# Two RWKV-7 buffers of a hybrid decoder kernel, run half a round apart

## The chip, the cores and the metric

One NeuronCore of a Trainium2 chip runs the whole program. The metric is device time in microseconds, the median of three runs. TensorE multiplies matrices, VectorE, ScalarE and GpSimd (POOL) work element by element, and each of them executes its own queue strictly in the order of the program. SyncE issues the weight transfers. The engines meet only through semaphores: an instruction that waits holds up everything behind it on its engine.

## What is computed

A decoder trunk of two layers on 256 prompt tokens and 8 sequences of 8 new tokens (T = 320 columns). The even layer has HGRN2 heads and RWKV-7 heads side by side; the change concerns the RWKV-7 heads alone. Per token:

```python
def rwkv7_scan(r, w, k, v, kk, a, s0):
    def step(s, inp):
        r_t, w_t, k_t, v_t, kk_t, a_t = inp
        sa = jnp.einsum('bhij,bhj->bhi', s, -kk_t)
        s = (s * w_t[:, :, None, :] + sa[..., None] * (kk_t * a_t)[:, :, None, :]
             + v_t[..., None] * k_t[:, :, None, :])
        return s, jnp.einsum('bhij,bhj->bhi', s, r_t)
```

Ahead of it stand the low-rank products for the decay, `a` and the gate (sigmoids), a normalised `kk` (square root and reciprocal) and exponentials; behind it a group norm (square root and reciprocal), a bonus term and the gate. There are 16 heads of 64; the last state of each head is written back for the prompt and for each of the 8 sequences.

## The kernel before

The program is written engine by engine. Weight products fill most of the time: every weight tile is split in a high and a low part (`split_hi`, `split_lo`, L280 and L291) and multiplied in three passes (L316, L320). Between the input projection of the even layer with its HGRN2 heads and the output projection `out_even` lies a stretch in which only the RWKV-7 heads run. This stretch is what the change touches.

The 16 heads are 8 tiles of two heads (128 partitions). Two tiles make a group (RJ = 2), there are four groups, and two sets of buffers, `rbuf[0]` and `rbuf[1]`, each with its own tiles, its own semaphores and four PSUM banks. A buffer does one group in one round, and two rounds in all. The 320 columns are five chunks of 64: four of the prompt, one that holds the eight sequences. One round of one buffer has 74 stages (RSTAGES):

- The front, stages 0 to 8. TensorE: low-rank products `lora` (L1237, L1238), sums of squares (L1244), bonus (L1249). ScalarE: sigmoids (L1005, L1006), square root (L1013), exponentials (L1017 to L1019). VectorE: a first block (L1093 to L1102), a block with a reciprocal (L1105 to L1107), four products that end in `tB` (L1111 to L1120). POOL: one product (L1222).
- Transposes and Gram products, stages 8 to 16. TensorE: 30 transposes (L1265), evacuated by ScalarE and VectorE in turns (L1074), then L1280 and L1277, masked by VectorE (L1129), and five operations that set up the inverse (L1138 to L1143).
- Five rungs of a triangular inverse, stages 16 to 36. A rung is a product (L1308), its copy to T1 by ScalarE (L1035), the next mask by VectorE (L1152), two more products (L1316, L1318; the fifth has L1316 alone) and additions by VectorE (L1158, L1161).
- Five chunks in sequence, stages 36 to 62. Each has three products on TensorE (`rhs` L1346, `sa` L1356, `ys` from L1365) with copies by ScalarE between them (L1046, L1049, L1053), and a state update by VectorE (L1172 to L1175). Ahead of the last one the states of the eight sequences are read (L1336).
- The tail, stages 62 to 74. New states of the sequences (L1378, L1380; VectorE L1183 to L1196), the group norm (L1387, L1393, square root L1065 on ScalarE, reciprocal L1206 on VectorE and what follows it up to L1214) and the gate (L1397).

Each engine's part is a generator (`rwkv_pe`, `rwkv_act`, `rwkv_dve`, `rwkv_pool`) that yields the stage of what it issues next. `by_stage` merges the generators of both buffers: it always takes the one with the lowest stage, and buffer 0 at a tie. As the stages of both buffers are equal, every step of buffer 0 is followed on its engine by the same step of buffer 1. The second round begins at stage 74 with a wait for the buffer's own `end` and, on ScalarE, for its stores (`rwkv_act`). After the stretch ScalarE and TensorE wait for the end of both buffers before `out_even` begins.

Of the kernel before, what the change touches and what calls it, by code (L numbers as in the profile page):

```python
# [109 lines left out]
def build(nc, d):  # L110
# [5 lines left out]
    with ctx:  # L116
# [282 lines left out]
        def part(ap, c):  # L399
            return ap[:, 2 * c:2 * c + 2, :]  # L400
# [140 lines left out]
        def by_stage(*programs):  # L541


            ahead = [[next(p, None), p] for p in programs]
            while any(a[0] is not None for a in ahead):
                a = min((a for a in ahead if a[0] is not None), key=lambda a: a[0])
                a[0] = next(a[1], None)


        HG, HGROUPS, HSTAGES = 2, 4, 21  # L550
        hK = at("hK", HT0, [P, HG, T])
# [665 lines left out]
        def rwkv_pool(pool, x):  # L1217
            r = rbuf[x]
            for G in range(RGROUPS // 2):
                yield G * RSTAGES + 6  # L1220
                r.wait(pool, "b", G + 1)
                pool.tensor_tensor(r.tB[:, :, :], r.KK[:, :, :], r.A[:, :, :], mult).then_inc(r.sem("kka"), 1)  # L1222
# [553 lines left out]
        @block.sync  # L1776
        def _(sp):
            for name in ORDER:
                ring_load(sp, plan[name])

        @block.gpsimd
        def _(pool):
            split_head(pool, "pool", plan["in_a"])
            pre_norm_pool(pool, FILL[0])
            pool_split(pool, plan["in_a"], skip=HEAD)
            in_b_pool(pool)
            by_stage(rwkv_pool(pool, 0), rwkv_pool(pool, 1))
            split_head(pool, "pool", plan["out_even"])
            mixer_x_pool(pool, FILL["mix0"])
            pool_split(pool, plan["out_even"], skip=HEAD)  # L1790
            split_head(pool, "pool", plan["up00"])
            post_norm_pool(pool, 1)
            channel_pool(pool, 0, plan["in_c"])
            pre_norm_pool(pool, FILL[4])
            pool_split(pool, plan["in_c"], skip=HEAD)
            pool_split(pool, plan["in_d"])
            split_head(pool, "pool", plan["out_odd"])
            mixer_x_pool(pool, FILL["mix1"])
            pool_split(pool, plan["out_odd"], skip=HEAD)
            split_head(pool, "pool", plan["up10"])  # L1800
            post_norm_pool(pool, 5)
            channel_pool(pool, 1, None)

        @block.scalar
        def _(act):
            act.dma_start(com[:, :], d["common"]).then_inc(sem("com_in"), 16)
            for c in range(8):
                act.dma_start(part(X, c), d["x"][:, 2 * c:2 * c + 2]).then_inc(sem(f"x_in{c}"), 16)
            act.dma_start(vecs[:, :], d["vecs"]).then_inc(sem("vecs_in"), 16)
            act_head(act, plan["in_a"])  # L1810
            act.wait_ge(sem("com_in"), 16)
            pre_norm_act(act, 0)

            for dst, src in ((hgm_in[:, :, :], "hgm"), (evc[:, :], "evc"), (sh_in[:, :, :], "shift_in")):
                act.dma_start(dst, d[src]).then_inc(sem("even_consts"), 16)
            act_split(act, plan["in_a"], skip=HEAD)
            by_stage(fill_act(act), hgrn_act(act))
            shift_act(act)
            by_stage(rwkv_act(act, 0), rwkv_act(act, 1))
            for r in rbuf:  # L1820
                act.wait_ge(r.sem("end"), 2)
                act.wait_ge(r.sem("store"), 64)
            act_head(act, plan["out_even"])
            mixer_x_act(act)
            act.wait_ge(sem("stored"), 16)
            act.dma_start(X[:, :, :], d["x"]).then_inc(sem("x_reload"), 16)
            act_split(act, plan["out_even"], skip=HEAD)
            act_head(act, plan["up00"])
            root_act(act, 1)
            channel_act(act, 0)  # L1830
            act_head(act, plan["in_c"])
            root_act(act, 3)
            pre_norm_act(act, 4)

            act.dma_start(x_spill, X[:, :, :]).then_inc(sem("spilled"), 16)
            act.wait_ge(sem("spilled"), 16)
            for dst, src in ((odc[:, :], "odc"), (cv_in[:, :, :, :], "conv_in"), (h_in[:, :, :], "h_in"),
                             (w_a[:, :, :, :], "w_a"), (w_x[:, :, :, :], "w_x")):
                act.dma_start(dst, d[src]).then_inc(sem("odd_consts"), 16)
            act_split(act, plan["in_c"], skip=HEAD)  # L1840
            by_stage(odd_fill_act(act), rglru_act(act))
            ret_act(act)
            act.wait_ge(sem("mix1_end"), 1)
            act_head(act, plan["out_odd"])
            mixer_x_act(act)
            act.wait_ge(sem("stored"), 16 * 3)
            act.dma_start(X[:, :, :], x_spill).then_inc(sem("x_reload"), 16)
            act_split(act, plan["out_odd"], skip=HEAD)
            act_head(act, plan["up10"])
            root_act(act, 5)  # L1850
            act.wait_ge(sem("ret_store3"), 32)
            channel_act(act, 1)
            root_act(act, 7)
            for c in range(8):
                x_new_wait(act, 7, c)
                act.dma_start(d["y"][:, 2 * c:2 * c + 2], part(X, c)).then_inc(sem("stored"), 16)
            act.wait_ge(sem("stored"), 16 * 11)
            act.wait_ge(sem("hgrn_store"), 32 * HGROUPS)

        @block.vector  # L1860
        def _(dve):
            split_head(dve, "dve", plan["in_a"])
            dve.wait_ge(sem("vecs_in"), 16)
            pre_norm_dve(dve, 0, ("mix_pre", 0), FILL[0])
            evacuate(dve, plan["in_a"], Z, skip=HEAD)
            dve.wait_ge(sem("even_consts"), 16 * 3)
            link(dve, "dve", dve.tensor_copy(hgm[:, :, :], hgm_in[:, :, :]))
            for g in range(HGROUPS):
                hgrn_dve(dve, g)
            dve.wait_ge(sem("shifted"), 26)  # L1870
            by_stage(rwkv_dve(dve, 0), rwkv_dve(dve, 1))
            pass_over(dve, plan["in_b"])
            split_head(dve, "dve", plan["out_even"])
            x_lo_dve_half(dve, mixer_part, FILL["mix0"])
            evacuate(dve, plan["out_even"], M, stats=1, skip=HEAD)
            split_head(dve, "dve", plan["up00"])
            post_norm_dve(dve, 1, ("mix_post", 0))
            channel_dve(dve, 0, plan["in_c"])
            pre_norm_dve(dve, 4, ("mix_pre", 1), FILL[4])
            evacuate(dve, plan["in_c"], Z[:, 32:48, :], skip=HEAD)  # L1880
            rglru_dve(dve)
            rotate_dve(dve)
            ret_dve(dve)
            pass_over(dve, plan["in_d"])
            split_head(dve, "dve", plan["out_odd"])
            x_lo_dve_half(dve, mixer_part, FILL["mix1"])
            evacuate(dve, plan["out_odd"], M, stats=33, skip=HEAD)
            split_head(dve, "dve", plan["up10"])
            post_norm_dve(dve, 5, ("mix_post", 1))
            channel_dve(dve, 1, None)  # L1890

        @block.tensor
        def _(pe):
            pe.wait_ge(sem("com_in"), 16)
            pre_norm_pe(pe, 0)
            multiply(pe, plan["in_a"], x_hi, x_lo, FILL[0])
            pe.wait_ge(sem("tile_out"), 32)
            by_stage(fill_pe(pe), hgrn_pe(pe))
            pe.wait_ge(sem("tile_out"), EVEN_TILES)
            pe.wait_ge(sem("hgrn_end"), HGROUPS)  # L1900
            pe.wait_ge(sem("lora_in"), 1)
            pe.wait_ge(sem("lora_w"), 32)
            by_stage(rwkv_pe(pe, 0), rwkv_pe(pe, 1))
            for r in rbuf:
                pe.wait_ge(r.sem("end"), 2)
            multiply(pe, plan["out_even"], x_hi, x_lo, FILL["mix0"])
            post_norm_pe(pe, 1)
            channel_pe(pe, 0)
            pre_norm_pe(pe, 4)
            multiply(pe, plan["in_c"], x_hi, x_lo, FILL[4])  # L1910
            pe.wait_ge(sem("tile_out"), plan["in_d"].tile0)
            by_stage(odd_fill_pe(pe), rglru_pe(pe))
            ret_pe(pe)
            pe.wait_ge(sem("mix1_end"), 1)
            multiply(pe, plan["out_odd"], x_hi, x_lo, FILL["mix1"])
            post_norm_pe(pe, 5)
            channel_pe(pe, 1)
# [93 lines left out]
```

## Time and profile before

| | us |
|---|---|
| median of the runs shown | 3699.97 (3682.28 to 3700.11, n = 3) |
| span of the profiled execution | 3677.0 |
| RWKV-7 stretch in it, first `lora` product to the end | 608.04 to 921.50 |

The span runs from the first to the last instruction; the profile gives no other time of that execution, and the runs are measured outside it. A row of the windows below gives busy time and, in brackets, the instructions of TensorE's products, its weight loads, VectorE, ScalarE and POOL, then the share of full speed that TensorE's clock was granted (1.00 is 2.4 GHz, 0.50 is 1.2 GHz), the DMA share and GB/s. In the timeline an instruction's row is its start, its length, engine, line, operation, what it writes and reads, shape and count, and in brackets the idle time of its engine before it with what ended that.

### The profile page before, as it was taken

What the parts mean: (1) busy time and instruction counts of PE and PEld (TensorE: products, weight loads), DVE (VectorE), ACT (ScalarE), POOL (GpSimd) and SP (SyncE); (2) the same over time, 40 slices, a digit from 0 to 9 for tenths busy, and PEclk for the clock granted to TensorE, in tenths of its full rate; (3) what the DMA queues carried; (4) which work ended last, traced back from release to release, by engine and by line L of the source; (5) the groups of instructions that cost most, each with busy time, mean ns of one, the idle gap of its engine ahead of it and who ended that gap; (6) DMA issues with size and microseconds to landing.
All of it is one profiled execution on the core that took longest, in us unless ns stands there. A gap on an engine that the chain in (4) does not pass through costs nothing.

```text
span 3677.0 us, 63816 instructions
## 1 busy us (share of the span) xinstructions
PE 3407.4 (93%) x24784; PEld 3270.7 (89%) x24784; DVE 1678.0 (46%) x2251; ACT 1169.2 (32%) x1384; POOL 1643.6 (45%) x1038
## 2 busy tenths in 40 slices
PE   7998896857879999999999799998979999999997
PEld 7998885846879999999999699985979999999997
DVE  3236667485563332233334546814563332233345
ACT  3244443231333332233322235421233332233322
POOL 4556773000444444544444455721444445444443
PEclk9999997978889999999999899986989999999999
DMA  5443331000424444444443444542424444444442
GB/s 166 151 150 111 122 105 55 4 24 15 153 88 149 148 150 159 137 149 148 148 159 133 148 145 124 173 144 120 145 91 148 148 155 154 137 149 148 155 150 107
DMA packets 118658, 474.81 MB, mean 129 GB/s; under 512 B 13425, under 2 KB 15089, under 8 KB 115569
## 3 DMA queue, kind: packets, MB, share of 16 engines
q1 hardware_dynamic: 108864, 421.58, 35.8%
q10 hardware_dynamic: 9648, 51.17, 3.6%
q8 instruction: 107, 1.75, 0.2%
q14 instruction: 39, 0.31, 0.0%
HBM read 450.66 MB, written 22.03 MB: 129 GB/s over the span
## 4 chain that ended last, share of the span: by engine, by line
PE 86%; DVE 9%; ACT 2%; issue 1%; POOL 1%; DMA 1%; ACTq 0%; DVEq 0%; POOLq 0%
PE ps L316 50%; PE ps L320 25%; DVE M L462 1%; PE ps L1719 1%; PE ps L1739 1%; DVE xn L425 1%; PE ps L837 1%; PE ps L1316 1%; POOL x_lo L433 1%; PE ps L418 0%; PE ps L1318 0%; PE ps L1280 0%; DVE Z L718 0%; PE ps L1265 0%; PE ps L1482 0%
## 5 line engine op out<-in xcount | busy, mean ns | idle before, releaser
L291 POOL TENSOR_TENSOR w_lo<-raw,w_hi 128x512 fp32r<-128x512 f32 (+2 forms) x756 | 1463.6, 1937 | 1734.7 <-ACT w_hi L280 1733.9
L316 PE MATMUL ps<-x_hi,w_hi 128*128 128x320 f32 x5024 | 1515.7, 315 | 89.8 <-POOL x_lo L433 71.8
L316 PE MATMUL ps<-x_lo,w_hi 128*128 128x320 f32 x5024 | 1504.1, 313 | 0.0
L280 ACT ACTIVATE w_hi<-raw 128x1024 fp32r<-128x1024 f32 (+1 forms) x756 | 840.8, 1113 | 1654.3 <-PE ps L320 1618.2
L316 PEld LDWEIGHTS ps<-x_hi,w_hi 128*128 128x128 f32 x5024 | 959.8, 191 | 107.9 <-issue 73.6
L291 DVE TENSOR_TENSOR w_lo<-raw,w_hi 128x512 fp32r<-128x512 f32 (+1 forms) x640 | 515.8, 807 | 1030.0 <-ACT w_hi L280 1012.1
L316 PEld LDWEIGHTS ps<-x_lo,w_hi 128*128 128x128 f32 x5024 | 961.8, 191 | 0.6
L320 PE MATMUL ps<-x_hi,w_lo 128*128 128x320 f32 x5024 | 846.4, 311 | 1.9 <-POOL w_lo L291 1.9
L320 PEld LDWEIGHTS ps<-x_hi,w_lo 128*128 128x128 f32 x5024 | 769.5, 189 | 2.9 <-POOL w_lo L291 2.9
L316 PE MATMUL ps<-u_hi,w_hi 128*128 128x320 f32 x1408 | 415.5, 310 | 6.3 <-DVE u_lo L530 6.3
L316 PE MATMUL ps<-u_lo,w_hi 128*128 128x320 f32 x1408 | 415.1, 309 | 0.0
L316 PEld LDWEIGHTS ps<-u_hi,w_hi 128*128 128x128 f32 x1408 | 264.4, 188 | 7.3 <-DVE u_lo L530 7.3
L316 PEld LDWEIGHTS ps<-u_lo,w_hi 128*128 128x128 f32 x1408 | 264.4, 188 | 0.0
L320 PE MATMUL ps<-u_hi,w_lo 128*128 128x320 f32 x1408 | 227.4, 309 | 0.0
L320 PEld LDWEIGHTS ps<-u_hi,w_lo 128*128 128x128 f32 x1408 | 211.8, 188 | 0.0
L530 DVE TENSOR_TENSOR u_lo<-stat,u_hi 128x320 f32 (+1 forms) x88 | 131.8, 1498 | 10.1
L523 DVE TENSOR_TENSOR stat<-gate,ps 128x320 f32<-128x320 f32 x88 | 42.9, 488 | 172.2 <-PE ps L320 172.2
L510 ACT ACTIVATE gate<-ps 128x320 f32<-128x320 f32 x88 | 38.5, 437 | 221.1 <-PE ps L320 221.1
L343 DVE COPY M<-ps 128x320 f32 (+1 forms) x64 | 31.5, 492 | 157.4 <-PE ps L320 157.4
L1222 POOL TENSOR_TENSOR tB<-rKK,rA 128x640 f32<-128x640 f32 x4 | 6.5, 1619 | 191.4 <-DVE rKK L1107 191.4
L418 PE MATMUL ps<-sq,com 128*128 128x320 f32 x128 | 46.9, 527 | 38.7 <-ACT sq L408 38.7
L418 PEld LDWEIGHTS ps<-sq,com 128*128 128x128 f32 x128 | 28.1, 231 | 57.0 <-ACT sq L408 36.5
(359 smaller groups left out, 2606.9 us busy)
## 6 DMA issues: line engine op xcount, KB each, us to landing
raw<-in_w_ffn_in SPq DMA_DIRECT2D x352, 512.0 KB, 3.5
raw<-in_w_ffn_out SPq DMA_DIRECT2D x128, 704.0 KB, 4.0
raw<-in_w_in_even SPq DMA_DIRECT2D x116, 512.0 KB, 3.5
raw<-in_w_in_odd SPq DMA_DIRECT2D x96, 512.0 KB, 3.5
raw<-in_w_out_even SPq DMA_DIRECT2D x32, 512.0 KB, 3.5
raw<-in_w_out_odd SPq DMA_DIRECT2D x32, 512.0 KB, 3.5
hS<-in_state_hgrn ACTq DMA_DIRECT2D x4, 1024.0 KB, 5.5
out_hgrn_s<-hS ACTq DMA_DIRECT2D x4, 1024.0 KB, 4.9
```

The costliest lines, as they stand in the source:

```text
L280: nc.scalar.activation(w_hi[s % 2][:, 0:g.kt, :], raw[s % 4][:, 0:g.kt, :], ACT.Copy)\
L291: eng.tensor_tensor(w_lo[s % 2][:, k0:k1, :], raw[s % 4][:, k0:k1, :], w_hi[s % 2][:, k0:k1, :].bitcast(f32), sub).then_inc(sem(f"split_lo ...
L316: nc.tensor.matmul(out, w_hi[s % 2][:, k, :], x[:, kk, :], start=half == 0 and k == 0 and x is xh, stop=False)
L320: mm = nc.tensor.matmul(out, w_lo[s % 2][:, k, :], xh[:, half * g.kt + k, :], start=False, stop=half == 1 and k == g.kt - 1)
L418: ins = nc.tensor.matmul(PS[7][:, 0:T], ones, sq[:, k, :], start=k == 0, stop=k == KT - 1)
L425: ins = dve.scalar_tensor_tensor(xn[:, k, :], X[:, k, :], vec(w[0], KT * w[1] + k), stat[:, 1, :], mult, mult)
L433: eng.tensor_tensor(part(x_lo, c), src, part(x_hi, c).bitcast(f32), sub)\
L462: ins = dve.scalar_tensor_tensor(M[:, k, :], M[:, k, :], vec(w[0], KT * w[1] + k), stat[:, 1, :], mult, mult)
L510: nc.scalar.activation(gate[:, p % 2, :], PS[(g.tile0 + 2 * p) % 4][:, 0:T], ACT.Silu)\
L523: dve.tensor_tensor(uf, gate[:, p % 2, :], PS[(g.tile0 + 2 * p + 1) % 4][:, 0:T], mult)\
L530: dve.tensor_tensor(lo, uf, hi.bitcast(f32), sub).then_inc(sem("u_lo"), 1)
L837: ins = mm(PS[b0][:, o:o + P], x[:, j, cs], x[:, j, cs], start=True, stop=True)
```

## The change

`by_stage` itself stays. The generators of the RWKV-7 stretch are wrapped in `paced`, which turns a stage into a position on a scale of 115 units per round, by straight lines between the points of PACE, and adds half a round (57.5) to all positions of buffer 1. Stage 0 is at 0, stage 8 at 21, 16 at 33, 36 at 63, 62 at 95, 74 at 115. All four engines are merged by these positions. No instruction, tile, wait or semaphore is added or removed.

```diff
+        PACE = ((0, 0), (8, 21), (16, 33), (36, 63), (62, 95), (74, 115))
+
+        def paced(program, late):
+
+            for stage in program:
+                G, n = divmod(stage, PACE[-1][0])
+                k = max(k for k, (first, _) in enumerate(PACE[:-1]) if first <= n)
+                (n0, t0), (n1, t1) = PACE[k], PACE[k + 1]
+                yield late * PACE[-1][1] / 2 + G * PACE[-1][1] + t0 + (n - n0) * (t1 - t0) / (n1 - n0)
...
-            by_stage(rwkv_pool(pool, 0), rwkv_pool(pool, 1))
+            by_stage(*(paced(rwkv_pool(pool, x), x) for x in range(2)))
...
-            by_stage(rwkv_act(act, 0), rwkv_act(act, 1))
+            by_stage(*(paced(rwkv_act(act, x), x) for x in range(2)))
...
-            by_stage(rwkv_dve(dve, 0), rwkv_dve(dve, 1))
+            by_stage(*(paced(rwkv_dve(dve, x), x) for x in range(2)))
...
-            by_stage(rwkv_pe(pe, 0), rwkv_pe(pe, 1))
+            by_stage(*(paced(rwkv_pe(pe, x), x) for x in range(2)))
```

## Rows read from the trace of the kernel before

**Rows 1.** The page: span, and shares of the chain that ended last.

```profile
span 3677.0 us, 63816 instructions
PE 86%; DVE 9%; ACT 2%; issue 1%; POOL 1%; DMA 1%; ACTq 0%; DVEq 0%; POOLq 0%
```

**Rows 2.** Windows: from:to and length, then the columns above; front, Gram, stretch.

```profile
608.04:637.88 29.84, 10.36 (x32) 5.80 (x32) 25.11 (x34) 12.67 (x22) 3.21 (x2) 0.61 0.09 30
637.88:662.22 24.34, 19.60 (x300) 18.66 (x301) 20.16 (x38) 7.77 (x20) 0.00 (x0) 0.92 0.01 1
608.04:921.50 313.46, 222.26 (x4136) 189.60 (x4136) 200.40 (x321) 81.33 (x187) 6.48 (x4) 0.83 0.05 15
```

**Rows 3.** Waits of TensorE in the stretch: who, us in total, times, longest.

```profile
PE ps L1265 <- DVE tB L1120: 33.1, 2, 16.7
```

**Rows 4.** Timeline of VectorE in the front of round 1.

```profile
617.21 0.68 DVE L1093 TENSOR_SCALAR tAR<-rA,vecs 128x320 f32<-128x320 f32 x2
622.02 0.49 DVE L1105 TENSOR_SCALAR rE<-rE 128x640 f32<-128x640 f32 x1
627.48 0.48 DVE L1105 TENSOR_SCALAR rE<-rE 128x640 f32<-128x640 f32 x1
632.93 1.68 DVE L1111 TENSOR_TENSOR BV<-ps,Z 128x320 f32<-128x320 f32 x4
```

**Rows 5.** Chain of waits, round 1 (start, us, what): transposes, Gram products, last rung.

```profile
637.88 8.39 PE ps L1265 x60
...
649.97 2.62 PE ps L1280 x48
652.59 0.93 PE ps L1277 x32
...
655.50 1.77 PE ps L1280 x32
...
698.99 1.88 PE ps L1316 x64
```

**Rows 6.** Timeline of the rungs of round 1.

```profile
666.40 2.40 PE L1308 MATMUL ps<-XI,NTm 64*64 64x64 f32 x40 [1.77 <-DVE XI L1143]
668.84 0.77 ACT L1035 ACTIVATE T<-ps 128x512 f32<-128x512 f32 x2 [3.41 <-PE ps L1308]
...
672.73 0.69 DVE L1158 TENSOR_TENSOR XT<-XT,ps 128x512 f32<-128x512 f32 x1 [3.06 <-PE ps L1318]
...
674.13 0.28 DVE L1161 TENSOR_TENSOR XI<-XI,ps 128x128 f32<-128x128 f32 x1
...
676.96 1.38 PE L1308 MATMUL ps<-XI,NTm 64*64 64x64 f32 x40 [0.77 <-DVE XI L1161]
...
684.97 1.15 PE L1308 MATMUL ps<-XI,NTm 64*64 64x64 f32 x32 [1.00 <-DVE XI L1161]
```

**Rows 7.** Windows, columns as in the second group: rungs before and after the clock rose, tail.

```profile
662.22:672.02 9.80, 8.03 (x145) 7.84 (x147) 5.67 (x7) 1.53 (x4) 0.00 (x0) 0.50 0.01 2
672.02:701.00 28.98, 26.00 (x859) 25.51 (x857) 16.74 (x32) 5.12 (x10) 0.00 (x0) 1.00 0.01 4
731.00:756.87 25.87, 17.08 (x104) 8.92 (x100) 19.87 (x30) 5.37 (x10) 0.00 (x0) 0.90 0.12 47
```

**Rows 8.** Chain of waits, round 1: state products, the last VectorE block of either buffer.

```profile
722.31 6.58 PE ps L1336 x122
...
749.19 4.16 DVE ySQ L1206
...
756.82 4.07 DVE ySQ L1206
```

**Rows 9.** Timeline of ScalarE: first and last of seven table loads, and an activation.

```profile
615.30 1.28 ACT L1013 ACT_TABLE_LOAD   x1
616.59 1.42 ACT L1013 ACTIVATE rE<-ps 128x320 f32<-128x320 f32 x4
...
904.04 1.28 ACT L1065 ACT_TABLE_LOAD   x1
```

## The prediction

> **What bounds the kernel now.** I read the page first: the chain that ended last lies on TensorE for 86% of a span of 3677.0 us [rows 1], so this is a kernel bound by its weight products. The change touches none of them, only the RWKV-7 stretch, so I then read that stretch by windows: it runs from the first lora product at 608.04 to 921.50, 313.5 us, and TensorE is busy for 222 of them, VectorE for 200 [rows 2]. Neither is full: a round of both buffers is some 157 us, with TensorE busy 111 and VectorE 100. The wait view tells where the difference goes: TensorE stands for 33.1 us in two waits for `tB`, the last operation of the front [rows 3], while VectorE does reciprocals; in the rungs it is VectorE's turn to wait. So the stretch alternates between a front of 29.84 us on VectorE (25.11 busy), and rungs on TensorE (26.00 of 28.98 at the full clock) [rows 2, 7]. Running one buffer's front beside the other's rungs is then a fair idea; the question is what a single buffer's chain costs and what the merged queues let it do.
>
> **How I sum.** In the new order the buffers' steps are sorted by PACE positions on every engine. Buffer 1's first product (L1237, stage 1) has position 57.5 + 2.6 = 60.1; buffer 0's fifth rung has 58.5 (L1308, stage 33) and 61.5 (L1316, stage 35). So on TensorE's queue buffer 1 starts right behind L1308 of buffer 0's last rung. Half a round on, the same three positions come with the roles exchanged (116, 117.6, 119), and again at 173.5 and 175.1. TensorE executes in order, therefore each half-round is at least as long as one buffer's path from its lora products to its fifth rung. Call it S, and E what is left behind that, from the fifth rung to the end. The stretch is S alone, three times S with the other buffer's E put between its steps (S + x), and E alone: **4 S + 3 x + E**, against 313.5 us now. The two halves of PACE's round look equal on paper; the sum asks for S, not for their mean.
>
> **S, one buffer alone.** Front: 29.84 us for both [rows 2]. Of buffer 1's VectorE work two blocks lie in it ahead of buffer 0's next step, from 617.21 to 622.02 (4.81) and from 627.48 to 632.93 (5.45) [rows 4]; without them 19.6. Transposes and Gram products: 24.34 us [rows 2], of which half of the 8.39 us of transposes and buffer 1's Gram products, 2.62 + 0.93 + 1.77 = 5.3, are the other buffer's [rows 5]: 14.8. Rungs: one is L1308 (1.38 us), the copy of T1 on ScalarE (0.77), 80 products of L1316 and L1318 at 1.88 / 64 = 0.029 us (2.35) [rows 5], four additions on VectorE from 672.73 to 674.41 (1.7) [rows 6]; with some 0.5 for the hand-overs 6.7 us. The third and fourth have 8 blocks in place of 10 and one bank, 5.4 (an estimate by these rates); with L1308 of the fifth, 2 x 6.7 + 2 x 5.4 + 1.2 = 25.4. **S = 19.6 + 14.8 + 25.4 = 60** at the full clock. The telling comparison is here: a rung of both buffers takes 8.0 us (676.96 to 684.97 for buffer 1's second) [rows 6], hardly more than one of a single buffer. Lockstep already hides the hand-overs of one buffer under the products of the other.
>
> **The clock.** After the idle time ahead of the first rung the rows show a granted clock of 0.50 (1.2 GHz) for 9.8 us, in which TensorE was busy for 8.03; then 1.00 (2.4 GHz) while it was busy nine tenths of the time [rows 7]. L1308 takes 2.40 us at the lower level, 1.38 at the higher [rows 6], a factor of 1.74. Alone, a rung has TensorE busy for 3.7 of its 6.7 us, a smaller share than in either of these rows, so I expect the first S to run at the lower level in part. Its 15 us of rung products would grow by 11, the transposes and Gram products by up to 8: S lies between 60 and 79, and I take 70 for the first. In the shared halves TensorE has more to do, and I keep 60.
>
> **x, what the other buffer adds.** Its E lies between the steps of S, in order on every queue. Nothing (0) if all of it falls into idle time, all of E (47) if nothing does. By place: (1) its last VectorE block, from 749.19 to 756.82, 7.6 us [rows 8], has position 111.7, ahead of the fourth rung's additions (114.5); those are ready some 3 us into it, so 4.5. (2) Its tail has 17.08 / 2 = 8.5 us of products [rows 7] spread over rungs 1 to 3, which leave TensorE idle for 3 us each; but each step waits in order for its own additions or copies: 4. (3) Chunks 3 and 4 and the state products (6.58 / 2 = 3.3 us for L1336 [rows 8]) stand among transposes, Gram products and the first rung, where TensorE is itself on the chain: 7.5 us of products, of which 6.5 count. (4) Chunks 0 to 2 beside the front: VectorE's state updates and the first waits, 3. **x = 18**, between 12 and 24.
>
> **E alone.** The rest of the fifth rung 2.5; four chunks at 4.4 (both buffers take (722.31 - 701.00) / 4 = 5.3 [rows 7, 8]; one is three products with two copies and an update between them, all in line, so nearer to 5.3 than to its half); state products 3.3, chunk 4 3.5, the tail 20 (25.87 up to buffer 0's end [rows 7], less some 6 for buffer 1's products and updates between its own). 47 at the full clock; with its 22 us of products at the lower level 63. I take 53.
>
> **Smaller edits.** ScalarE now loads an activation table seven times in the stretch, 1.28 us each [rows 9], because the two buffers share each load of sigmoid, square root and exponential. Half a round apart they don't: by the order of the positions 14 loads, 9.0 us more. A load is issued ahead of the wait of its activation, so most are hidden by that wait; I count 4, between 0 and 9. Beside it, and for nothing in the sum: the Trainium skill (ScalarE: Activation LUTs, What ACT_TABLE_LOAD costs, and the rule there to do all of one table set before switching) speaks against the change, and puts a drain behind each load, 2.66 us in all; this trace disagrees on the size, the next activation starts 1.29 us after the load did [rows 9]. By its figure seven loads would be 18.6 us and not 9.0. Moved at no cost: POOL's `tB` (its queue holds nothing else in the stretch), and buffer 1's load of `state_rwkv`, which is issued later and wanted only at its first chunk, some 60 us on. In the second round ScalarE waits for buffer 0's end and its stores (position 115), with buffer 1's last T1 copy (117.5) queued behind that, and L1316 waits for the copy; on TensorE those products (119) stand behind buffer 0's next lora products and the same wait anyway, so no term is added.
>
> **The sum.** 70 + 3 x (60 + 18) + 53 + 4 = 361 us against 313.5: +47.5 us. I take **+50**, for the sum leaves out the lower clock in the shared fronts. The profiled execution would span 3727 us; the page gives its span alone, which lies 23 us under the median of the runs, 3699.97 (they run from 3682.28 to 3700.11), so on that median **3750 us**.
>
> **Rivals.**
> Overlap wins, faster. Fronts run beside rungs, and x falls to idle time. At the full clock, without table loads, the stretch is 4 x 60 + 47 + 3 x = 287 + 3 x: it breaks even at x = 8.8, and at x = 0 ends 26.5 us sooner, 3673 on that median. For it: TensorE and VectorE together are busy for 422 of 2 x 313.5 us. Against it: blocks (1) and (3) alone are 11, and the position puts them on the chain. The Trainium skill (Perfetto Trace Analysis, Optimization Strategy) says that where the most-contended engine changes, interleaving such regimes may help; this trace has such regimes, and no run here shows yet that the merged order pays.
> Even. The clock stays full in the lone stretches and x is 8 to 13: 311 to 326 and the loads, within 0.5% of now, some 3700 to 3715.
> The clock decides. Both lone stretches and the rungs in the shared halves at the lower level: 79 + 3 x 84 + 63 + 9 = 403, +90, 3790.
> That the change leaves the order as it is can be ruled out: positions differ by 57.5 from the first stage on.
>
> **How the numbers follow.** The forecast has 0.72, the clock rival 0.12, even 0.12, overlap wins 0.04. Terms at their lower ends: 60 + 3 x 72 + 47 = 323, +10, 3710. At their upper ends in the lone parts, x at 24: 79 + 3 x 86 + 63 + 9 = 409; all of these at once is unlikely, and I cut at +85. Range 3712 to 3785. About 0.5%, 18.5 us, is what a measurement of this kernel can tell from no change. So faster by more 0.04, within it 0.12, slower by more 0.84.
>
> **What would show it.** Buffer 1's first L1237 near 675, not 610; three further distances between first L1237s of near 78 us; E alone some 50 at the end, with ScalarE's table loads at 14. The chain of waits would show VectorE's L1206 ahead of L1158 in the rungs, and TensorE at 0.50 in the first rungs. The prediction is wrong if those distances are under 68 us: then the merged queues hide what I put on the chain.

## The result, and the profile after

The change makes the kernel slower. After: 3757.65 us, median of 4 runs (3748.02 to 3762.19); before: 3691.14 us, median of 4 (3682.28 to 3700.11). The ratio is 1.018, with a 95% interval from 1.015 to 1.0211, so +66.5 us. The order of before, in which the two buffers go step by step side by side, is called lockstep here; a part of the stretch in which only one buffer is at work is called lone. In code and rows of after, all lines of the RWKV-7 programs are 10 higher than before: L1237 is L1247, L1308 is L1318, L1206 is L1216.

The span of after, from its page, against 3677.0 us [rows 1]:

```profile
span 3760.4 us, 63820 instructions
```

The span grew by 83.4 us, but not all of that is the change (last section). The stretch is compared by its own ends, first lora product to last instruction: 377.7 us against 313.5 [rows 2], **+64.2**.

Windows of after, columns as in [rows 2]. First buffer 0 alone up to its fifth rung, by part (front; transposes and Gram products; rungs), then the second half-round by the same parts, then the five parts of the stretch and its whole:

```profile
609.60:629.70 20.10, 6.83 (x16) 3.69 (x17) 14.26 (x19) 7.73 (x12) 1.54 (x1) 0.58 0.05 15
629.70:647.30 17.60, 12.13 (x150) 10.76 (x150) 10.56 (x18) 3.88 (x10) 0.00 (x0) 0.79 0.01 2
647.30:682.60 35.30, 25.51 (x466) 24.11 (x466) 9.52 (x18) 2.73 (x6) 0.00 (x0) 0.58 0.06 16
...
682.60:705.30 22.70, 13.01 (x177) 10.16 (x176) 15.91 (x23) 11.05 (x20) 1.55 (x1) 0.82 0.00 1
705.30:727.60 22.30, 20.34 (x344) 19.00 (x342) 11.63 (x22) 5.71 (x17) 0.00 (x0) 0.88 0.01 2
727.60:763.40 35.80, 25.57 (x522) 20.43 (x519) 22.98 (x36) 6.14 (x12) 0.00 (x0) 0.88 0.10 33
...
609.60:682.60 73.00, 44.48 (x632) 38.56 (x632) 34.34 (x55) 14.33 (x28) 1.54 (x1) 0.63 0.04 12
682.60:763.40 80.80, 58.92 (x1037) 49.59 (x1036) 50.52 (x81) 22.90 (x49) 1.55 (x1) 0.86 0.05 15
763.40:845.10 81.70, 60.27 (x1037) 50.17 (x1036) 50.53 (x81) 22.91 (x49) 1.54 (x1) 0.83 0.05 15
845.10:925.10 80.00, 58.52 (x1006) 48.42 (x1005) 49.84 (x79) 22.91 (x49) 1.54 (x1) 0.84 0.03 9
925.10:987.30 62.20, 43.65 (x436) 33.55 (x436) 16.37 (x26) 6.54 (x19) 0.00 (x0) 0.58 0.03 11
609.60:987.30 377.70, 265.83 (x4136) 220.29 (x4136) 201.59 (x322) 89.60 (x194) 6.17 (x4) 0.76 0.04 13
```

The product count is the same 4136 as before, and VectorE's busy time nearly the same (200.4 and 201.6 us). What grew is TensorE's idle time, from 91.2 to 111.9 us, and its busy time, from 222.3 to 265.8, with the same products at a mean granted clock of 0.76 in place of 0.83. Most of these 43.6 us lie in the lone parts: S and E together keep TensorE busy for 88.1 us, where a quarter of the stretch of before, with about as many products, takes 55.6. How much of that lies on the chain is shown for S alone (third experiment).

The forecast's equation can be read straight from the windows: S 73.0, three shared halves of 80.8, 81.7 and 80.0, and E 62.2. Two shared halves are a round of both buffers, 161.7 to 162.5 us, where lockstep takes 149 to 157: the new order loses in the middle too, not at its ends alone.

TensorE's timeline in after: L1318 of the fourth and fifth rung of buffer 0 (674.61, 681.49) and of buffer 1 (750.62, 761.46), and the other buffer's first product behind either:

```profile
674.61 1.15 PE L1318 MATMUL ps<-XI,NTm 64*64 64x64 f32 x32 [1.47 <-DVE XI L1171]
...
681.49 1.15 PE L1318 MATMUL ps<-XI,NTm 64*64 64x64 f32 x32 [1.47 <-DVE XI L1171]
682.56 0.53 PE L1247 MATMUL ps<-Z,w2a 64*128 64x320 f32 x1
...
750.62 1.15 PE L1318 MATMUL ps<-XI,NTm 64*64 64x64 f32 x32
...
754.27 0.33 PE L1328 MATMUL ps<-T,XT 64*64 64x64 f32 x4
761.46 1.97 PE L1318 MATMUL ps<-XI,NTm 64*64 64x64 f32 x32 [6.87 <-DVE XI L1171]
763.37 0.90 PE L1247 MATMUL ps<-Z,w2a 64*128 64x320 f32 x1
```

L1247 starts as L1318 ends, and its rows show no wait of their own: its place in the queue is what it waited for. This is the chain on which the forecast rests.

VectorE's timeline in after, the second half-round, around the fourth rung's additions:

```profile
751.89 0.69 DVE L1162 TENSOR_TENSOR NTm<-G,evc 128x512 f32<-128x512 f32 x1 [2.22 <-PE ps L1318]
752.50 4.15 DVE L1216 RECIPROCAL ySQ<-ySQ 128x640 f32<-128x640 f32 x1
...
760.04 0.68 DVE L1168 TENSOR_TENSOR XT<-XT,ps 128x512 f32<-128x512 f32 x1
760.63 0.68 DVE L1171 TENSOR_TENSOR XI<-XI,ps 128x512 f32<-128x512 f32 x1
```

Buffer 0's last block (L1216 up to L1224) stands ahead of buffer 1's additions: the products that these add up end at 754.60 (754.27 + 0.33), and the additions start at 760.04, 5.4 us later. That is the larger part of the wait of 6.87 us at 761.46 above; a lone rung waits 1.47. Before, TensorE's great wait was for `tB`, 33.1 us [rows 3]. The waits of TensorE in the stretch of after (who for whom, us in total, times, longest):

```profile
PE ps L1318 <- DVE XI L1171: 31.5, 10, 6.9
PE ps L1375 <- ACT SA L1059: 21.5, 11, 6.2
PE ps L1275 <- DVE tB L1130: 10.7, 1, 10.7
```

The front's wait has left, except in the lone start. In its place are waits inside the chains: chunks for their copies, and rungs for their additions, 31.5 us in 10 waits, where lockstep had 6.0 in 8, as the same view of before shows:

```profile
PE ps L1308 <- DVE XI L1161: 6.0, 8, 1.0
```

### The profile page after: what moved, and what is told of

It reads as the page before. It is cut to its first block, busy times and chain, and to the rows that moved or that the text cites. A ratio compares the mean times of both kernels' runs of the same rounds, so it can differ in the third digit from the quotient of the medians.

```text
span 3760.4 us, 63820 instructions
## 1 busy us (share of the span) xinstructions
PE 3470.5 (92%) x24784; PEld 3315.1 (88%) x24784; DVE 1675.4 (45%) x2251; ACT 1177.9 (31%) x1391; POOL 1642.8 (44%) x1038
## 4 chain that ended last, share of the span: by engine, by line
PE 69%; DVE 3%; POOL 1%; issue 1%; DMA 0%; ACT 0%; ACTq 0%; DVEq 0%; POOLq 0%
PE ps L316 43%; PE ps L320 22%; PE ps L1729 1%; PE ps L1749 1%; DVE M L462 1%; DVE xn L425 1%; POOL x_lo L433 0%; PE ps L1492 0%; DVE stat L397 0%; PE ps L1736 0%; DVE X L453 0%; DMA x_spill<-X 0%; PE ps L418 0%; PE ps L1724 0%; PE ps L1744 0%
## 5 line engine op out<-in xcount | busy, mean ns | idle before, releaser
L343 DVE COPY M<-ps 128x320 f32 (+1 forms) x64 | 31.5, 492 | 157.2 <-PE ps L320 157.2
```

## Experiments

Durations of the stretch are from each kernel's profiled execution. Lengths of S, halves and E are distances on TensorE's queue from a first lora product to the next, or to the end of the fifth rung's L1318.

**One buffer after the other.** Buffer 1 begins when buffer 0 has done both its rounds, so that rounds stand nearly alone:

```diff
-                yield late * PACE[-1][1] / 2 + G * PACE[-1][1] + t0 + (n - n0) * (t1 - t0) / (n1 - n0)
+                yield late * 240 + G * PACE[-1][1] + t0 + (n - n0) * (t1 - t0) / (n1 - n0)
```

> Buffer 1 is put 240 units behind buffer 0, more than both of its rounds: the buffers run one after the other, and every round is a lone one. Nothing else changes. Theory (a lone buffer's chain costs nearly as much as a round of both, and runs with TensorE at 1.2 GHz for most of it): a lone round is S + E = 73 + 62 = 135 us as in the changed kernel's first and last stretches, the whole RWKV-7 stretch about 4 x 135 = 530 to 540 us, S at each start within 3 us of 73. Rival (a lone round is as short as PACE has it, 115, or as my S and E at the full clock, 107, and what costs is only the merging of the queues): 430 to 460 us.

Measured: 3910.27 us beside 3695.63 for before. Windows: the first round, its S and its E, and the stretch:

```profile
613.70:744.30 130.60, 82.64 (x1036) 68.17 (x1036) 50.19 (x80) 22.18 (x48) 1.54 (x1) 0.64 0.02 8
613.70:684.20 70.50, 41.98 (x630) 36.43 (x630) 33.66 (x53) 14.35 (x28) 1.54 (x1) 0.69 0.02 6
684.20:744.30 60.10, 40.67 (x407) 31.74 (x406) 16.53 (x27) 7.83 (x20) 0.00 (x0) 0.59 0.03 11
613.70:1136.70 523.00, 334.14 (x4136) 276.32 (x4136) 202.12 (x322) 92.67 (x195) 6.18 (x4) 0.63 0.03 9
```

TensorE's timeline of before shows how long a round of lockstep is: buffer 1's first lora product, then that of either buffer in the second round:

```profile
610.30 0.74 PE L1237 MATMUL ps<-Z,w2a 64*128 64x320 f32 x1
...
756.87 0.90 PE L1237 MATMUL ps<-Z,w2a 64*128 64x320 f32 x1 [7.47 <-DVE Z L1214]
...
764.41 0.90 PE L1237 MATMUL ps<-Z,w2a 64*128 64x320 f32 x1 [5.04 <-DVE Z L1214]
```

A round of one buffer takes 131 to 134 us. (Only the second is shorter by this measure, 126, as buffer 1's first product starts there ahead of buffer 0's last VectorE block.) A lockstep round of both takes 149 for buffer 0 (608.04 to 756.87) and 154 and 157 for buffer 1 (610.30 to 764.41, and on to 921.5). So one buffer's round costs about five sixths of two buffers' (130.6 / 154.1 is 0.85); its S is 70 to 74 in all four rounds and its E 60, but for 53 in the second. The rival, that the rounds alone would give 430 to 460, falls: lockstep was already hiding one buffer under the other. Not all of the five sixths is hand-overs: the lone rounds are granted 0.61 to 0.65, lockstep 0.83 [rows 2]. With the added products of the third experiment S and E come to 63.8 and 59.6 at 0.82 and 0.76, which is still 0.80 of 154.1.

**A quarter of a round, and a few per cent.** The same change with a smaller lag. For the second, PACE is also set to the times at which lockstep reaches these stages:

```diff
-                yield late * PACE[-1][1] / 2 + G * PACE[-1][1] + t0 + (n - n0) * (t1 - t0) / (n1 - n0)
+                yield late * PACE[-1][1] / 4 + G * PACE[-1][1] + t0 + (n - n0) * (t1 - t0) / (n1 - n0)
```

```diff
-        PACE = ((0, 0), (8, 21), (16, 33), (36, 63), (62, 95), (74, 115))
+        PACE = ((0, 0), (8, 10.2), (16, 21.8), (36, 75.7), (62, 108.2), (74, 141.7))
...
-                yield late * PACE[-1][1] / 2 + G * PACE[-1][1] + t0 + (n - n0) * (t1 - t0) / (n1 - n0)
+                yield late * 7.2 + G * PACE[-1][1] + t0 + (n - n0) * (t1 - t0) / (n1 - n0)
```

> The changed kernel with buffer 1 a quarter of a round behind (28.75 units) instead of a half; PACE as it is. Theory (what is lost grows with the part of the chain that a buffer runs without its partner in the same stage): the first lone stretch is about 38 us, a lone end of 40, the whole stretch between the two kernels, 340 to 350 us. Rival (half a round is right and only the merging of that one order costs): worse than half a round, over 378; or no loss at all, 313.

> Buffer 1 runs 7.2 units behind buffer 0, about one VectorE block of a round of 142 units, with PACE = ((0, 0), (8, 10.2), (16, 21.8), (36, 75.7), (62, 108.2), (74, 141.7)). Theory (lockstep's gain, hand-overs of one buffer under products of the other, is kept by a small lag, and buffer 1's blocks no longer stand between buffer 0's in the front and at the end of a round): the stretch gets 5 to 12 us shorter than the 313.4 us of the kernel before, 301 to 308, the whole time 0.1 to 0.3% less. Rival (any lag takes the buffers apart and adds waits in order): 318 us or more.

Measured, a quarter: 3749.17 us. Windows, buffer 1's lead and the stretch:

```profile
616.50:648.30 31.80, 17.78 (x168) 13.56 (x168) 20.83 (x34) 11.34 (x21) 1.55 (x1) 0.69 0.06 15
616.50:972.10 355.60, 249.98 (x4136) 207.20 (x4136) 201.81 (x323) 89.58 (x194) 7.34 (x4) 0.81 0.04 14
```

The stretch was forecast at 340 to 350 and came out at 355.6. Buffer 1 starts 31.8 us late, its first round takes 176.2 us (154.1 in lockstep) and its last 147.6 (157.0): 29.5 + 22.1 - 9.4 = +42.2 us. With half a round the lead is 73.0 us, the rounds 162.5 and 142.2: 70.7 + 8.4 - 14.8 = +64.3. At half, the lead is given back by 14.8 us only, because the late buffer's last round, which ends alone, hardly becomes shorter: a lone round is not much shorter than a shared one. At a quarter the middle of the stretch pays more, 22.1 us; why is not shown.

Measured, 5%: 3675.42 us in 10 runs (3669.57 to 3688.70), before 3687.92 in 25 (3672.29 to 3716.00), ratio 0.9969 with a 95% interval from 0.9944 to 0.9994: a gain that its interval just separates from nothing. Window of the stretch:

```profile
609.10:918.20 309.10, 233.47 (x4136) 196.33 (x4136) 202.72 (x323) 89.31 (x193) 6.24 (x4) 0.83 0.05 16
```

Waits of TensorE in it:

```profile
PE ps L1275 <- DVE tB L1130: 19.0, 2, 9.9
PE ps L1290 <- DVE nat L1084: 13.2, 4, 5.8
```

The wait for `tB` falls from 33.1 us [rows 3] to 19.0, as wished, and 13.2 us of a new wait, of the Gram products for VectorE's copies of the transposes (L1084), give nearly all of it back; the stretch gains 4.4 us (309.1 against 313.5), where 5 to 12 were forecast.

**Extra products that keep TensorE busy in the lone stretches.** Products whose results nobody reads, on after: 19 in buffer 0's first Gram part and rungs, 15 between buffer 1's last chunks. (The edit also lets those last chunks wait for buffer 0's end, as they write into its bank; buffer 0 is done by then.)

```diff
+            def keep_warm(n):
+                for _ in range(n):
+                    mm(other[3][:, 0:T], ones, rscan, start=True, stop=True)
...
                     ins.then_inc(r.sem("xu"), 1)
+                    if first and l < 5:
+                        keep_warm(2)
```

> The changed kernel with extra products of constants by constants on TensorE, into a PSUM bank of the other buffer that nobody uses then: 6 behind buffer 0's first Gram products, 3 per rung in its first round, and 3 per chunk in buffer 1's last round (0.54 us each at 2.4 GHz). Their results are not read. Theory (the lone stretches are long because the clock falls to 1.2 GHz): granted clock in the first S rises from 0.63 to over 0.8 and S falls from 73 to about 62 us; E alone falls from 62 to about 52; the shared halves stay at 81; the stretch goes from 378 to about 357. Rival (the lone stretches are hand-overs between engines, the clock matters little): S and E get longer by what the extra products add, 74 to 78 and 63 to 68, the stretch 380 or more.

Measured: 3737.77 us beside 3695.63; stretch 368.3. Windows, S and E:

```profile
609.10:672.90 63.80, 46.61 (x668) 35.40 (x668) 34.34 (x55) 14.93 (x29) 1.54 (x1) 0.82 0.05 15
917.80:977.40 59.60, 47.11 (x466) 31.57 (x466) 16.52 (x27) 6.54 (x19) 0.00 (x0) 0.76 0.03 11
```

The group of the added products within E, from the view by lines:

```profile
L1242 PE MATMUL ps<-evc,com 128*128 128x320 f32 x30 | 14.9, 585 | 0.0
```

S falls from 73.0 to 63.8 us although more products lie in it, and the granted clock rises from 0.63 to 0.82. The lone S without added products takes 70.3 to 73.8 us in the other traces, so at least 6.5 us of it were the lower clock, 9.2 in after's own. E falls by 2.6 only; here 14.9 us of added products stand in line between chunk steps that wait for each other, so this run doesn't tell what the clock costs in E. The three halves are 2.4 us longer in all (242.5 and 244.9). Of the 64.2 us lost, 54.8 remain, with E still at 0.76 and 357 forecast for the stretch: the clock of S is a smaller part of the loss, and that of E stays open.

**The last block without its reciprocal.** L1216 is left out, on after and, as the control, on before.

```diff
-                L(dve.reciprocal(r.YSQ[:, :, :], r.YSQ[:, :, :]))
```

> The changed kernel without the reciprocal in the tail (L1206 of before, 4.15 us on VectorE): the group norm then multiplies by the deviation instead of dividing. Theory (that block stands ahead of the other buffer's fourth-rung additions and delays the chain in each shared half): each of the three shared halves gets 4 us shorter, 81 to 77, and the end 4.15 shorter, the stretch 16 us shorter, 378 to 362. Rival (in the shared halves the block falls into idle time): only the end gets shorter, the stretch 374.

> The kernel before without the same reciprocal. In lockstep both buffers' blocks stand one after the other between the last products of a round and the next round's first, so both theories expect 4 x 4.15 = 16.6 us less, 313 to 297. Beside e3 this gives what a VectorE operation of the tail costs in either order.

Measured: on after 3745.24 us, stretch 361.3 (-16.4); on before 3662.54, stretch 294.7 (-18.8). VectorE's timeline of the first, at the place shown above for after:

```profile
752.68 0.69 DVE L1162 TENSOR_TENSOR NTm<-G,evc 128x512 f32<-128x512 f32 x1 [2.22 <-PE ps L1317]
753.29 0.82 DVE L1216 TENSOR_TENSOR rY<-rY,ySQ 128x640 f32<-128x640 f32 x1
...
757.24 0.68 DVE L1171 TENSOR_TENSOR XI<-XI,ps 128x512 f32<-128x512 f32 x1
```

TensorE's fifth rung behind it:

```profile
758.07 1.47 PE L1317 MATMUL ps<-XI,NTm 64*64 64x64 f32 x32 [2.68 <-DVE XI L1171]
```

(L1216 is here the line behind the one left out, and L1317 is L1318 of after.) From L1162 to the last addition it is now 4.56 us (752.68 to 757.24), against 8.74 in after (751.89 to 760.63), and the fifth rung's product follows the fourth's after 6.7 us in place of 10.8 (750.62 to 761.46). In this place the reciprocal costs some 4 us, as forecast. What is left of the block still costs something: the wait is 2.68 us, in a lone rung 1.47. (A lone rung of after takes 6.9 us, 674.61 to 681.49, but at a granted 0.75 against 1.00 here, so the like length says nothing of the block.) The three halves, though, fall by 1.0, 4.5 and 3.0 us only, 8.5 of some 12, so a part is given back elsewhere in the half (in the first, the granted clock is 0.82, in after 0.86). And 2.7 of the 16.4 are no gain of this edit: they lie in the first S (70.3 us at 0.69), ahead of any such block. In lockstep the stretch without the four reciprocals is 18.8 us shorter, 4.7 each, where 16.6 were forecast: there they stand on the way to the next round and to the end.

**Table loads.** Square root and exponential are taken as sigmoid in the RWKV-7 programs, so that ScalarE loads no table in the stretch; on after and on before.

```diff
-                    ins = act.activation(r.E[:, j, :], bank[j][:, 0:T], ACT.Sqrt)
+                    ins = act.activation(r.E[:, j, :], bank[j][:, 0:T], ACT.Sigmoid)
...
-                act.activation(r.tAR[:, 1], r.tK[:, :, :], ACT.Exp, scale=WLOG_SCALE)
+                act.activation(r.tAR[:, 1], r.tK[:, :, :], ACT.Sigmoid, scale=WLOG_SCALE)
```

> The changed kernel with sigmoid in place of square root and exponential in the RWKV-7 stretch, so that ScalarE needs no other activation table there: what is computed changes, the work does not. Theory (loads are issued ahead of the waits and mostly hidden): 14 loads of 1.28 us go, the stretch gets 4 to 9 us shorter, 378 to 369 to 374. Rival (the loads that were added explain a good part of the loss, each on the chain): 18 us shorter or more, 360 or less.

> The same in the kernel before, 7 loads. Theory: 3 to 6 us shorter, 313 to 307 to 310, so that the two kernels stay some 62 us apart without any load. Rival (loads are on the chain in both): 9 us shorter.

The other three such lines are changed in the same way. Measured: 3761.67 us and 3684.93, beside 3697.42 for before. Window of the stretch, first of after with one table:

```profile
609.20:986.80 377.60, 266.22 (x4136) 220.32 (x4136) 201.53 (x322) 71.33 (x180) 6.17 (x4) 0.76 0.04 13
```

then of before with one table:

```profile
613.60:922.20 308.60, 218.96 (x4136) 187.98 (x4136) 200.26 (x321) 72.42 (x180) 6.50 (x4) 0.84 0.05 16
```

After loses 14 loads (18 us of ScalarE's busy time) and 0.1 us of its stretch, where 4 to 9 were forecast. Before loses 7 and 4.9 us. These are one execution each, and the lone S alone differs by up to 3.5 us between executions. So the change doubled the loads and hid them, as far as this can tell, where lockstep seems to have paid for some: the loads explain none of the loss.

**Extra products in lockstep.** If the lower clock ahead of the rungs [rows 7] costs lockstep time, unread products in VectorE's waits should bring it back; on before, and on the 5% lag.

```diff
+                yield at0 + 16
+                w("n", G + 1)
+                for _ in range((3, 5)[x]):
+                    mm(bank[3][:, 0:T], ones, rscan, start=True, stop=True)
```

Four or six more stand ahead of the transposes, added in the same way.

> The kernel before, in lockstep, with extra products of constants on TensorE into the buffer's own free bank: 6 and 4 once each buffer's reciprocal block is done, 3 and 5 ahead of the first rung. Their results are not read. Theory (the clock that falls to 1.2 GHz while TensorE waits costs time in lockstep too, as the rungs' first 9.8 us and the transposes run at it): granted clock in a round rises from 0.84 to over 0.92, each round gets 4 to 6 us shorter, the stretch 313 to about 303. Rival (those products are not on the chain, or the extra ones are): 312 or more.

> The small lag of the other run and the extra products together. Theory: the two gains add, as one is VectorE's and the other TensorE's clock: stretch about 293 to 300 us, whole time 0.4 to 0.5% below the kernel before. Rival (the lag spreads the products, so that the clock holds without the extra ones): no better than the small lag alone.

Measured: on before 3686.77 us, ratio 0.9993, interval from 0.9965 to 1.002, stretch 310.9; on the 5% lag 3697.33, ratio 1.0006, from 0.998 to 1.0033, stretch 315.3. Neither gains against before. Beside the 5% lag alone the products even cost 21.9 us (3697.33 and 3675.42; the runs of the two don't overlap); 6.2 of these lie in the stretch, and the rest isn't explained. TensorE's timeline of the first, added products and the first rung of either buffer:

```profile
662.99 4.57 PE L1304 MATMUL ps<-evc,com 128*128 128x320 f32 x16
667.79 1.38 PE L1316 MATMUL ps<-XI,NTm 64*64 64x64 f32 x40 [0.23 <-DVE XI L1143]
671.96 2.40 PE L1316 MATMUL ps<-XI,NTm 64*64 64x64 f32 x40 [2.79 <-DVE XI L1143]
```

Buffer 0's first rung is at the higher level now (1.38 us), but buffer 1's waits 2.79 us for VectorE, which sets up its inverse in line behind buffer 0's, and takes 2.40 us again, as before [rows 6]. In this row the rung waits for VectorE, and a faster TensorE ahead of it only waits longer. The gain of 10 us forecast for these products did not come.

## Why the prediction was right, by its steps

- **The queue's order sets the half-rounds: right, and seen.** L1247 of one buffer follows L1318 of the other's fifth rung without a gap, and buffer 1's first product stands at 682.56, where about 675 was forecast. This step carries the sign. The forecast took distances under 68 us for the sign of being wrong; with S and E as measured, the stretch would have got shorter only with distances under 59.4 ((313.5 - 73.0 - 62.2) / 3).
- **S: mechanism right, size low by 3.** Forecast 70, measured 73.0; by part 20.1, 17.6 and 35.3 against 19.6, 14.8 and 25.4 at the full clock. The excess over these is mostly in the rungs, at a granted 0.58; with products added S is 63.8 at 0.82, so the 60 of a full clock is near. The same S took 70.5 and 70.3 in two other runs, both at 0.69. The forecast expected the lower clock because a lone rung keeps TensorE busy for a smaller share of the time; the last section has a row against that reason.
- **Shared halves: 78 forecast, 80.8, 81.7 and 80.0 measured.** By place in the second half-round: front 22.7 (19.6 + 3 forecast), transposes and Gram products 22.3 (14.8 + 6.5), rungs 35.8 (25.4 + 4.5 + 4). The first two fit within 1 us, the rungs are 1.9 longer, with the clock at 0.88 there, not full as assumed. x, from S and a shared half at nearly the same clock: 81 - 63.8 = 17, forecast 18. Its term for VectorE's last block, 4.5, is 5.4 at its place in the trace; the reciprocal's share of it is some 4 there, and 1.0 to 4.5 by the length of the halves. Over three halves this step missed 8.5 us.
- **E: the step that was mis-sized most.** Forecast 53, between 47 and 63; measured 62.2 at a granted 0.58, next to the upper end. The term was 47 at the full clock and 63 at the lower level, and I took a value between them; the trace grants E 0.58, near the lower level. What share is clock and what hand-overs stays open, since the added products lay in E's own queue.
- **Table loads: 4 forecast, 0.1 measured.** There are 14, as the positions said, each 1.28 us. In ScalarE's timeline of after the load for buffer 1's first activation stands beside its lora products, which TensorE runs from 682.56 on:

```profile
683.28 1.28 ACT L1015 ACT_TABLE_LOAD   x1
684.58 0.53 ACT L1015 ACTIVATE rWB<-ps,vecs 128x320 f32<-128x320 f32 x1
```

  The Trainium skill (ScalarE: Activation LUTs, What ACT_TABLE_LOAD costs) adds a drain to each load. This trace shows none, as in before: the next activation starts 1.30 us after the load did, and without its loads the changed kernel is no faster.
- **The sum.** 361 forecast for the stretch, 377.7 measured: +3, +8.5, +9, -4 by the four terms. I had rounded +47.5 up to +50 for the clock in the shared fronts; +64.2 came. The measured halves with 60 and 47 for S and E, the forecast's values at the full clock, would give 349.5, +36: by this estimate the order of the queues makes somewhat over half of the loss and the lower clock of the lone parts the rest. A run shows only 6.5 to 9.2 us of that rest, in S; no run shows the 47. The median lies nearer to the forecast (3757.65 against 3750) than the stretch does, and that is luck: the median of before beside it is 3691.14, not the 3699.97 to which I added.
- **The rivals.** Overlap wins and even both needed x under 13: it was 17. The clock rival's mechanism was there nearly in full in S's rungs and in E (0.58) and in part in the halves (0.83 to 0.86), so the truth lies between forecast and that rival (403). The Trainium skill (Perfetto Trace Analysis, Optimization Strategy) says that interleaving regimes may help; of the three lags run here, half a round cost 64 us, a quarter 42, and 5% gave 4.

## What to carry to other kernels

Before setting two buffers apart, compare one buffer's round alone with a round of both: where the first is a chain (here five sixths of the second), lockstep is already the overlap, and a lag is paid in full at the start and hardly given back at the end. On engines that execute in order, merging two programs by positions also merges their chains: find which instruction of the one stands right behind which of the other, and take that distance, not the mean of the busy times, as the length of a half. Beside it look at the granted clock of the lone parts: here the lone parts ran near the lower level (0.63 in S, 0.58 in E). A lag of a few per cent that fills one named wait is the safer form, and even that gave nearly all of its gain to the next wait here.

## What the runs showed of the hardware

The span grew by 83.4 us, 64.2 of which lie in the stretch. 16.7 of the rest lie in the retention stage, whose code the change doesn't touch. The windows of it, of before:

```profile
2440.00:2555.20 115.20, 110.44 (x386) 74.81 (x385) 43.77 (x53) 8.86 (x18) 0.00 (x0) 0.68 0.23 93
```

and of after:

```profile
2507.00:2638.90 131.90, 127.08 (x385) 85.76 (x385) 43.81 (x54) 8.92 (x18) 0.00 (x0) 0.59 0.20 82
```

The same products take 16.7 us longer at a granted clock of 0.59 in place of 0.68. Whether that is chance or comes of the change is not shown. The runs of before differ by steps of that size among themselves (3682 and 3700), and the medians leave only 2.3 us outside the stretch (66.5 against 64.2). But in the twelve kept traces the stage's 256 products of L1719 (L1729 in after) take 93 us in before and in before without the reciprocal, 104 to 105 in the five others that are in lockstep, at a 5% lag or with added products, and 116 to 119 in after, one after the other, the quarter, and after without the reciprocal and with one table. So the stretch is taken by its own ends, and whole times of single runs tell less.

The other thing that I had not expected is how far the lone chains stay at the lower level. In the lone rungs TensorE is busy for 25.51 of 35.30 us and is granted 0.58, in E for 43.65 of 62.20 and is granted 0.58 too; in the rungs of lockstep it is busy for 26.00 of 28.98 and is granted 1.00 [rows 7]. The busy share alone doesn't tell them apart: in the rungs of a shared half, where the other buffer's products stand in between, TensorE is busy for 25.57 of 35.80 and is granted 0.88.
